# Two-layer hybrid network and mixture-of-experts block on one core: the conditioning vectors made by VectorE from a transposed modulation matrix instead of by TensorE

## The chip, the cores and the metric

One core of a Trainium2 chip runs the whole program. The metric is the device time in microseconds, median of three runs.

## What is computed

A first block of two hybrid layers (a convolution branch, a latent attention branch and a dilated attention branch, merged by gates) acts on x, 256 tokens of 1024 features. A second block follows: attention over tokens and a context, both modulated, then 32 experts of which each token uses four. All values are fp32. The change touches only how the modulation of the second block is made:

```python
mod_x = (jax.nn.silu(c) @ w_ada[l] + b_ada[l])[:, None, :]
mod_c = (jax.nn.silu(c_ctx) @ w_ada[l] + b_ada[l])[None, None, :]
sh1, sc1, gt1, sh2, sc2, gt2 = jnp.split(mod_x, N_MOD, axis=-1)
csh1, csc1, cgt1, csh2, csc2, cgt2 = jnp.split(mod_c, N_MOD, axis=-1)
h = modulate(rms_norm(x, g_attn[l]), sh1, sc1)        # h * (1 + sc1) + sh1
hc = modulate(rms_norm(ctx, g_attn[l]), csh1, csc1)
...
x = x + gt1 * (lat_mix @ w_o[l])
x = x + gt2 * moe_ffn(modulate(rms_norm(x, g_ffn[l]), sh2, sc2), ...)
```

c and c_ctx are vectors of 1024, w_ada is 1024 x 6144. The result does not depend on x, so it can be made at any time before the second block. Of c_ctx only the first 2048 columns (csh1, csc1) are used.

## The kernel before

Five engines run programs of their own, ordered by semaphores. SyncE (SP) issues all loads.

**The layers.** A layer is a list of units (UNITS). A weight tile of 2 MB is loaded into a ring of two slots, and cut into four quarters. ScalarE rounds a quarter into w_hi (L2037, `split_to`), GpSimd subtracts to get w_lo (L2138), and TensorE then runs three products (hi x hi, lo x hi, hi x lo, L1749 and L1759, `quarter`). Three quarters are buffered (PARTS), so a buffer is rounded anew as soon as TensorE has left it. Units up to PREP make the projections for the attentions: lora, dq, dk, dv, z, with the short latent units mq and mkv between them. VectorE normalizes and rotates their results (`normalize`, `rotate`, L2185 to L2188), TensorE turns them (`turn`, L1784), ScalarE copies them out of PSUM (`unflip`). ScalarE and VectorE wait for each other in these steps (squares, mean, root, reciprocal; "copied" for mkv).

**The jobs.** Twelve attention jobs follow (JOBS: four latent, eight dilated, j = 0 to 11). In step j TensorE makes the scores of job j (L1800, L1801, L1812), then waits for the probabilities of job j-1 (`values`, L1826 transposes, L1843 products) and between these runs quarters of the remaining weight tiles (`fill`). VectorE masks the scores of job j and takes the maximum (`mask`, L2357 to L2382), ScalarE does the exp (`exp`, L1999 to L2004), VectorE divides (`divide`, L2388 to L2395), and that releases the transposes of job j in the next step. The dilated jobs with odd j (5, 7, 9, 11) have two score steps: a second mask stands between the first and the exp. ScalarE copies the turned probabilities (`unflip_probs`, L2016). VectorE also does the convolution at j = 3 and 4 (L2342, L2345) and takes finished units out of PSUM. After the jobs come the merge (L1726), the output projection and the next layer.

**The conditioning before the change.** silu of c and c_ctx lies in SBUF as columns (`silu`, 8 chunks of 128 x 2, padded to 32). In each layer eight units of kind "ada" take 256 columns of w_ada each (1 MB, loaded by SP, L1652) and `ada_rows` (L715) multiplies them, four chunks side by side in the TensorE array. The result is a row, which ScalarE copies to `modrow` (L1961). After the first step of the jobs `pick` (L722) turns all rows of the layer with 16 small products (two passes each) into the PSUM tile mixed, and VectorE copies them to `mod` (L2442). The last 2048 columns are made in the attention block: four tiles of 2 MB in the ring (L647), eight half units between the last eight jobs (L715), and a second `pick` behind them, before the spreading of the sub norm (L891). The attention block has sixteen jobs (scores L823, maximum, exp L1173, division L1377 to L1384, transposes L833, values L845, copy L1390) and runs quarters of the projections and of w_o2 between them (`bfill`).

The calls that the prediction follows, in VectorE's order in a layer:

```python
for u in range(PREP):
    evacuate(l, u)
for j in range(NJ + 1):
    if j < NJ:
        mask(l, j, 0)
    for u in DONE_IN[j - 1] if j else ():
        evacuate(l, u)
    if j < NJ and len(STEPS[j]) == 2:
        mask(l, j, 1)
    if j < NJ:
        divide(l, j)
```

## Time and profile before

| | |
|---|---|
| time, median of 3 runs | 1980.42 us (1977.73 to 1983.41) |
| span of the profiled execution | 1975.8 us, 4.6 us less than that median |
| busy: TensorE, VectorE, ScalarE, GpSimd | 1885.4, 739.3, 581.0, 523.6 us |
| mean DMA rate | 285 GB/s |
| layer 1, layer 2, attention block, experts | 0 to 408, 408 to 810, 810 to 1041, 1041 to 1976 us |

The span is that of one execution; what the runs measure beyond it lies before its first and behind its last instruction, and between executions. A busy TensorE is an engine with a matmul in it, not one at its peak. GpSimd works in the layers only.

### The profile page before, as it was taken

The numbers are of one execution on the slowest core, as the hardware profiler recorded it, in microseconds if no ns is written. First come the engines' busy times: TensorE is split into PE (matmuls) and PEld (weight loads), VectorE is DVE, ScalarE is ACT, GpSimd is POOL, SyncE is SP. The second block draws the span as 40 slices with busy tenths as digits, with TensorE's granted clock in tenths as the row PEclk, the third lists the DMA queues.
The fourth block names the chain that finished last, engine by engine and source line by source line (L and its number), as shares of the span: only waits on it lengthen the run. The fifth ranks groups of instructions, "written<-read, shape, count | busy, mean of one in ns | idle before, by whom it ended". The sixth has DMA issues, their size and how long they took to land.

```text
span 1975.8 us, 26971 instructions
## 1 busy us (share of the span) xinstructions
PE 1885.4 (95%) x10996; PEld 1196.5 (61%) x10996; DVE 739.3 (37%) x1358; ACT 581.0 (29%) x1059; POOL 523.6 (27%) x220
## 2 busy tenths in 40 slices
PE   7999999989999899999999999999999999999997
PEld 6779989977799799844584444334334443433443
DVE  4785563447854643643533122111112211211112
ACT  4554455445554554423421111111001110110111
POOL 5766556767765558200000000000000000000000
PEclk9999999999999999999989999999999999999999
DMA  8556323545553334621558999999999999999995
GB/s 306 192 172 212 128 96 123 213 170 198 201 173 130 125 129 170 216 94 43 213 231 355 428 429 428 429 429 429 428 429 428 428 428 428 429 428 429 429 428 233
DMA packets 111413, 563.43 MB, mean 285 GB/s; under 512 B 4768, under 2 KB 24352, under 8 KB 86464
## 3 DMA queue, kind: packets, MB, share of 16 engines
q1 hardware_dynamic: 111328, 562.21, 71.2%
q8 instruction: 63, 1.03, 0.2%
q14 instruction: 22, 0.18, 0.0%
HBM read 561.15 MB, written 1.05 MB: 285 GB/s over the span
## 4 chain that ended last, share of the span: by engine, by line
PE 64%; DMA 28%; DVE 5%; ACT 1%; issue 1%; SPq 0%; DVEq 0%; ACTq 0%
DMA ring<-in_e_in_dram 28%; PE bank L1759 15%; PE score L964 11%; PE bank L1749 10%; PE bank L765 5%; PE mixed L1002 4%; PE bank L1726 3%; PE bank L796 1%; PE mixed L1843 1%; PE flip L1826 1%; DVE ring L2345 1%; PE bank L1025 1%; PE score L985 1%; PE score L823 1%; PE flip L1784 1%
## 5 line engine op out<-in xcount | busy, mean ns | idle before, releaser
L2138 POOL TENSOR_TENSOR w_lo<-ring,w_hi 128x1024 fp32r<-128x1024 f32 (+1 forms) x216 | 523.4, 2435 | 282.5 <-ACT w_hi L2037 281.8
L964 PE MATMUL score<-ring,space 128*64 128x512 f32 x2016 | 452.7, 594 | 38.6 <-DMA ring<-in_e_in_dram 37.5
L964 PEld LDWEIGHTS score<-ring,space 128*64 128x64 f32 x2016 | 141.5, 137 | 338.7 <-issue 248.6
L2037 ACT ACTIVATE w_hi<-ring 128x1024 fp32r<-128x1024 f32 (+1 forms) x216 | 226.5, 1050 | 218.8 <-PE bank L1759 119.3
L1759 PE MATMUL bank<-h_hi,w_hi 128*128 128x256 f32 x896 | 261.7, 292 | 0.0
L1759 PE MATMUL bank<-h_lo,w_hi 128*128 128x256 f32 x896 | 254.1, 284 | 0.0
L1759 PE MATMUL bank<-h_hi,w_lo 128*128 128x256 f32 x896 | 253.9, 283 | 0.0
L1002 PE MATMUL mixed<-ring,space 128*64 128x512 f32 x1024 | 228.1, 598 | 0.0
L1229 ACT ACTIVATE space<-space 128x512 f32<-128x512 f32 x32 | 20.2, 632 | 697.0 <-DVE space L1533 697.0
L1533 DVE TENSOR_SCALAR space<-score 128x512 f32<-128x512 f32 x32 | 22.2, 693 | 411.3 <-PE score L964 411.3
L1759 PEld LDWEIGHTS bank<-h_hi,w_hi 128*128 128x128 f32 x896 | 172.4, 192 | 4.5 <-issue 4.4
L1759 PEld LDWEIGHTS bank<-h_lo,w_hi 128*128 128x128 f32 x896 | 172.5, 193 | 0.1
L1759 PEld LDWEIGHTS bank<-h_hi,w_lo 128*128 128x128 f32 x896 | 172.2, 192 | 0.0
L1002 PEld LDWEIGHTS mixed<-ring,space 128*64 128x64 f32 x1024 | 71.0, 137 | 133.7 <-issue 131.4
L1749 PE MATMUL bank<-w_hi,h_hi 128*128 128x512 f32 (+1 forms) x320 | 131.9, 412 | 7.6 <-DVE h_lo L2194 7.6
L1546 DVE COPY space<-mixed 64x512 f32<-64x512 f32 x32 | 21.9, 684 | 297.5 <-PE mixed L1002 297.5
L1749 PE MATMUL bank<-w_hi,h_lo 128*128 128x512 f32 (+1 forms) x320 | 125.4, 392 | 0.0
L1749 PE MATMUL bank<-w_lo,h_hi 128*128 128x512 f32 (+1 forms) x320 | 125.1, 391 | 0.0
L1749 PEld LDWEIGHTS bank<-w_hi,h_hi 128*128 128x128 f32 x320 | 61.3, 192 | 24.5 <-issue 12.1
L1749 PEld LDWEIGHTS bank<-w_hi,h_lo 128*128 128x128 f32 x320 | 61.4, 192 | 12.1
L1749 PEld LDWEIGHTS bank<-w_lo,h_hi 128*128 128x128 f32 x320 | 61.5, 192 | 11.7 <-issue 1.0
L765 PE MATMUL bank<-ring,h 128*128 128x512 f32 (+1 forms) x160 | 64.5, 551 | 0.6 <-ACT h L1112 0.6
(349 smaller groups left out, 2341.0 us busy)
## 6 DMA issues: line engine op xcount, KB each, us to landing
ring<-in_e_in_dram SPq DMA_DIRECT2D x126, 2048.0 KB, 25.1
ring<-in_e_out_dram SPq DMA_DIRECT2D x64, 2048.0 KB, 22.1
ring<-in_w_in_dram SPq DMA_DIRECT2D x42, 2048.0 KB, 7.8
ring<-in_w_ada_dram SPq DMA_DIRECT2D x16, 1024.0 KB, 5.4
ring<-in_w_o_dram SPq DMA_DIRECT2D x6, 2048.0 KB, 7.9
ring<-in_w_qkv_dram SPq DMA_DIRECT2D x4, 2048.0 KB, 11.3
ring<-in_w_ada_dram SPq DMA_DIRECT2D x4, 2048.0 KB, 8.1
ring<-in_w_out_a_dram SPq DMA_DIRECT2D x2, 2048.0 KB, 8.0
```

The source lines that it names most:

```text
L765: ins = pe.matmul(b[:, 0:n], src[:, c, tt * P:(tt + 1) * P], w8[:, c, 0:n], start=c == 0, stop=c == DC - 1)
L796: ins = pe.matmul(b[:, i * T:(i + 1) * T], w8[:, c, m:m + P], mix[:, c, :], start=c == 0 and i == 0, stop=c == DC - 1, skip_group_check=True)
L964: ins = pe.matmul(score[HALF * blk:HALF * blk + HALF, which * W:(which + 1) * W], xs[:, 2 * j + r, HALF * hh:HALF * hh + HALF], wk[:, blk ...
L1002: ins = pe.matmul(mixed[HALF * side:HALF * side + HALF, :], actT[:, hh, a * P + HALF * half:a * P + HALF * half + HALF], ring[:, 4 + half, ...
L1229: act.activation(tanh_g[:, hh, :], glu[:, hh, :], ACT.Tanh, scale=GLU_ALPHA / 2).then_inc(glu_tanh, 1)
L1533: dve.tensor_scalar(glu[:, hh, :], score[:, 0:W], GLU_LIMIT, None, ALU.min).then_inc(glu_free, 1)
L1546: dve.tensor_copy(ys[0:HALF, hh, :], mixed[0:HALF, :])
L1726: ins = pe.matmul(b[:, i * T:(i + 1) * T], w_[:, c, m], y_[br][:, c, :], start=c == 0 and i == 0 and y_ is y_hi and w_ is hi, stop=c == 3 ...
L1749: ins = pe.matmul(b[:, 0:n], x_[:, c, t], w_[:, k % PARTS, i, 0:n], start=c == 0 and x_ is h_hi and w_ is w_hi, stop=c == DC - 1 and x_ is ...
L1759: ins = pe.matmul(b[:, half * T:(half + 1) * T], w_[:, k % PARTS, i, m:m + P], x_[:, c, :], start=c == 0 and half == 0 and x_ is h_hi and ...
L2037: act.activation(split_part(w_hi, k), raw_part(k), ACT.Copy).then_inc(hi_done, 1)
L2138: pool.tensor_tensor(split_part(w_lo, k), raw_part(k), split_part(w_hi, k), ALU.subtract).then_inc(lo_done, 1)
```

## The change

c and c_ctx come from the host as rows of 1024, repeated in all 128 partitions; w_ada comes transposed, as 48 blocks of 128 x 1024. A column of `mod` is then one VectorE instruction: the product of a block with the silu row, summed along the row (`tensor_tensor_reduce`). Both conditions together need 64 such sums: each layer does 16 steps of two (1 MB loaded per step). The blocks of the first 2048 columns are loaded twice in the first layer, for c_ctx and for c; the second layer does the other 4096, so nothing is left for the attention block. One step stands right behind the norm of x at the head of a layer, five in PREP, ten in jobs 0 to 9. One buffer holds the 1 MB; the loads after the first of a layer are issued by ScalarE. The tanh of the rows is made by ScalarE at the head of each layer, behind the last piece of h_hi. The ada units, their PSUM copies, `pick`, and their loads are gone.

```diff
-ADA_AFTER = {1: 1, 3: 2, 5: 3, 7: 4, 9: 5, 10: 6, 11: 7}
-ADA_LOAD = {2: 1, 4: 2, 6: 3, 8: 4, 10: 5, 12: 6, 13: 7}
-UNITS = [("ada", None, (0,))]
+UNITS = []
...
+COND = 2
+ROWS = [[(1, COND * n) for n in range(8)] + [(0, COND * n) for n in range(8)], [(0, COND * n) for n in range(8, 24)]]
+NROWS = 16
+ROWS_AFTER = {LONG_AT[0] + 1: 1, LONG_AT[1] + 1: 2, LONG_AT[7] + 1: 3, LONG_AT[9] + 1: 4, PREP - 1: 5}
+ROWS_LOAD = {LONG_AT[0]: 1, LONG_AT[1]: 2, LONG_AT[3]: 3, LONG_AT[8]: 4, LONG_AT[10]: 5}
+ROWS_JOB = 6
+CTX_STEPS = 8
...
-BUNITS += [("ada", (7, 8, 11, 12)[n], (n,)) for n in range(4)]
...
-BHALVES = [4] + [2] * NGQA + [2] * 7 + [1]
+BHALVES = [4] + [2] * NGQA + [1] * 7 + [0]
...
-            pe.wait_ge(mixed_free, MIXED0 + M_ADA + 1)
-            for n in range(4):
-                pe.wait_ge(bank_free[BBANK[BADA + n]], bfreed(BADA + n))
-                ins = pick(pe, bmodrow[:, n, :], 8 * n)
-            ins.then_inc(mixed_done, 1)
...
+        def rows_of(l, k):
+            a = ROWS[l][k][1]
+            return w_ada[a:a + COND].rearrange("a p k -> p a k")
...
+                def first_rows(l):
+                    if l:
                         sp.wait_ge(free_of(MERGED - 1), freed(l - 1, MERGED - 1))
+                    sp.dma_start(c_row, c_in[:, 0:D]).then_inc(c_loaded, 16)
+                    if l == 0:
+                        sp.dma_start(ctx_row, c_in[:, D:2 * D]).then_inc(c_loaded, 16)
+                    sp.dma_start(ada_sb, rows_of(l, 0)).then_inc(ada_landed, 16)
...
@@ block.tensor, after the first step of the jobs @@
-                        pe.wait_ge(mixed_free, l * NM + 1)
-                        for n in range(ADAS):
-                            ins = pick(pe, modrow[:, n, :], 8 * n)
-                        ins.then_inc(mixed_done, 1)
...
@@ block.scalar @@
-            act.activation(tanh_z[:, 0:2 * DC], cvec[:].rearrange("p c b -> p (c b)"), ACT.Tanh,
-                           scale=0.5).then_inc(ctanh, 1)
+            def row_tanhs(l):
+                act.wait_ge(c_loaded, 32 if l == 0 else 48)
+                if l == 0:
+                    act.activation(row_tanh[:, 1, :], ctx_row, ACT.Tanh, scale=0.5).then_inc(ctanh, 1)
+                act.activation(row_tanh[:, 0, :], c_row, ACT.Tanh, scale=0.5).then_inc(ctanh, 1)
+            def load_rows(l, k):
+                act.wait_ge(ada_used, l * NROWS + k)
+                act.dma_start(ada_sb, rows_of(l, k)).then_inc(ada_landed, 16)
...
                     split_to(l, min(n + 1, PARTS))
                     stream_high(l, n, normed_x)
-                evacuate(l, 0)
-                for u in range(HEAD, PREP):
+                row_tanhs(l)
+                for u in range(PREP):
                     if u in QUARTER:
                         k = QUARTER[u]
                         for q in range(4):
                             split_to(l, k + q + 1 + PARTS)
                             if (u, q) in TURN:
                                 unflip(l, NORMED.index(TURN[u, q]))
+                        if u in ROWS_LOAD:
+                            load_rows(l, ROWS_LOAD[u])
                         evacuate(l, u)
...
                     if j > 0:
                         unflip_probs(l, j - 1, 0)
+                    if ROWS_JOB + j < NROWS:
+                        load_rows(l, ROWS_JOB + j)
                     if j < NJ and len(STEPS[j]) == 1:
                         exp(l, j)
...
@@ block.vector @@
+            def silu_rows(l):
+                for i, row in ((1, ctx_row), (0, c_row)):
+                    if i == 0 or l == 0:
+                        dve.wait_ge(ctanh, l + 2 - i)
+                        dve.scalar_tensor_tensor(out=row, in0=row_tanh[:, i, :], scalar=1.0, in1=row, op0=ALU.add,
+                                                 op1=ALU.mult).then_inc(row_ready, 1)
+                dve.wait_ge(row_ready, l + 2)
+            def use_rows(l, k):
+                b, a = ROWS[l][k]
+                dve.wait_ge(ada_landed, 16 * (l * NROWS + k + 1))
+                for i in range(COND):
+                    ins = dve.tensor_tensor_reduce(out=ada_sb[:, i, :], in0=ada_sb[:, i, :], in1=(c_row, ctx_row)[b],
+                                                   scale=0.5, scalar=0.0, op0=ALU.mult, op1=ALU.add,
+                                                   accum_out=mod[:, a + i, b:b + 1])
+                ins.then_inc(ada_used, 1)
...
+                silu_rows(l)
+                use_rows(l, 0)
                 for u in range(PREP):
                     evacuate(l, u)
+                    if u in ROWS_AFTER:
+                        use_rows(l, ROWS_AFTER[u])
                 for j in range(NJ + 1):
                     if j < NJ:
                         mask(l, j, 0)
                     for u in DONE_IN[j - 1] if j else ():
                         evacuate(l, u)
+                    if ROWS_JOB + j < NROWS:
+                        use_rows(l, ROWS_JOB + j)
                     if j < NJ and len(STEPS[j]) == 2:
                         mask(l, j, 1)
                     if j < NJ:
                         divide(l, j)
...
-                        dve.wait_ge(mixed_done, l * NM + 1)
-                        dve.tensor_copy(mod[:, bass.ds(l * 4 * ADAS, 4 * ADAS), :],
-                                        mixed[:, 0:8 * ADAS].rearrange("p (c b) -> p c b", b=2)).then_inc(mixed_free, 1)
```

## Rows read from the trace of the kernel before

**Rows 1.** Stages: busy us (instructions) of PE, PEld, DVE, ACT, POOL; PEclk, DMA share, GB/s.

```profile
60.00:160.00 100.00, 98.91 (x527) 77.42 (x526) 83.54 (x97) 51.31 (x81) 70.66 (x29) 1.00 0.56 190
...
1195.00:1485.00 290.00, 272.33 (x1333) 111.82 (x1333) 49.58 (x110) 29.19 (x64) 0.00 (x0) 1.00 1.01 429
```

**Rows 2.** Timeline of TensorE in PREP: start, us, line, operation [idle before].

```profile
41.80 1.07 PE L715 MATMUL mixed<-ring,silu 128*32 128x256 f32 x16
```

**Rows 3.** Timeline of TensorE: turning of the rows, and what follows it.

```profile
189.92 3.63 PE L722 MATMUL mixed<-cst,ring 128*128 128x2 f32 x32
...
195.18 1.06 PE L1826 MATMUL flip<-cst,space 128*128 128x128 f32 x4
...
996.11 6.58 PE L722 MATMUL mixed<-cst,space 128*128 128x2 f32 x32
```

**Rows 4.** Stages around the turning in both layers; the granted clock stands after POOL.

```profile
160.00:200.00 40.00, 39.81 (x331) 37.63 (x331) 17.41 (x29) 20.16 (x39) 23.88 (x11) 0.96 0.54 185
...
560.00:600.00 40.00, 39.81 (x318) 37.64 (x318) 17.88 (x26) 18.20 (x31) 24.75 (x11) 0.92 0.54 185
```

**Rows 5.** VectorE with two SBUF inputs (groups by line: xcount, busy, mean ns), then GpSimd.

```profile
L2213 DVE TENSOR_TENSOR latent_r<-space,latent_r 128x1024 fp32r<-128x1024 f32 x1 | 3.2, 3208 | 0.0
...
L2213 DVE TENSOR_TENSOR latent_r<-ring,latent_r 128x1024 fp32r<-128x1024 f32 x1 | 1.2, 1215 | 0.0
...
289.86 3.39 POOL L2138 TENSOR_TENSOR w_lo<-ring,w_hi 128x1024 fp32r<-128x1024 f32 x1
```

**Rows 6.** Timelines of ScalarE and GpSimd: table load, split at the head, 128x1024 operation.

```profile
2.40 1.28 ACT L1912 ACT_TABLE_LOAD   x1 [2.40 <-DMA cvec<-in_c_dram]
...
25.23 9.06 POOL L2138 TENSOR_TENSOR w_lo<-ring,w_hi 128x832 fp32r<-128x832 f32 x4 [3.14 <-ACT w_hi L2037]
...
279.12 1.05 ACT L2048 ACTIVATE latent_r<-space 128x1024 fp32r<-128x1024 f32 x1
```

**Rows 7.** DMA issues by line: xcount, KB each, median us from issue to landing.

```profile
ring<-in_w_ada_dram SPq DMA_DIRECT2D x16, 1024.0 KB, 5.4
```

**Rows 8.** Timeline of the first layer's jobs: transposes, copies, masks, divisions.

```profile
181.75 0.69 DVE L2295 SCALAR_TENSOR_TENSOR space<-ring,bank 128x512 f32<-128x512 f32 x1 [0.72 <-ACT ring L1984]
...
247.80 0.66 PE L1826 MATMUL flip<-cst,space 128*128 128x128 f32 x4
...
260.18 1.15 DVE L2395 TENSOR_SCALAR space<-space 128x768 f32<-128x768 f32 x2
...
261.82 0.66 PE L1826 MATMUL flip<-cst,space 128*128 128x128 f32 x4
...
275.03 0.66 PE L1826 MATMUL flip<-cst,space 128*128 128x128 f32 x4
...
280.07 0.59 ACT L2016 ACTIVATE space<-flip 128x512 f32<-128x512 f32 x1
...
282.05 0.75 DVE L2371 SCALAR_TENSOR_TENSOR space<-cst,score 128x256 f32<-128x256 f32 x2 [1.32 <-PE score L1812]
...
286.51 1.15 DVE L2395 TENSOR_SCALAR space<-space 128x768 f32<-128x768 f32 x2
...
289.47 0.66 PE L1826 MATMUL flip<-cst,space 128*128 128x128 f32 x4
...
302.67 0.66 PE L1826 MATMUL flip<-cst,space 128*128 128x128 f32 x4
...
314.88 0.66 PE L1826 MATMUL flip<-cst,space 128*128 128x128 f32 x4
```

**Rows 9.** Timeline of the attention block: scores, copy of the mixed rows, diagonal.

```profile
956.94 1.13 PE L823 MATMUL score<-space 64*128 64x512 f32 x4
...
962.40 1.13 PE L823 MATMUL score<-space 64*128 64x512 f32 x4
...
962.64 0.28 DVE L1390 COPY space<-mixed 128x128 f32<-128x128 f32 x1
...
997.03 1.29 DVE L1398 TENSOR_TENSOR space<-cst,space 128x512 f32<-128x512 f32 x2
```

142 lines of the change are left out of this document (41 added, 101 removed).

## The prediction

> **What bounds the kernel now.** I read the table of stages first, then the waits, then the timelines of single stretches. The span falls into two dense layers (0 to 408 us and 408 to 810), an attention block (810 to 1041) and 32 experts (1041 to 1976). In a layer TensorE is busy 98.9 of 100 us while the conditioning rows are made, and VectorE, second, is busy 83.5, GpSimd 70.7 [rows 1]. So there a microsecond taken from TensorE is a microsecond gained, if VectorE, GpSimd and ScalarE still deliver in time. Among the experts the DMA engines are full (429 GB/s) and TensorE waits for them [rows 1]; the first tile of the second expert is only asked for when TensorE has used the first one's, so whatever moves the start of the experts moves the end by as much, and nothing else there is touched by the change.
>
> **What is removed from TensorE.** Seven of a layer's eight products of 16 matmuls lie between full-rate work and cost 1.0 us each (1.07 less the overlap, [rows 2]): 7.0 us a layer. The eighth stands at the layer's head, where TensorE waits for h_lo anyway: 0. The 32 small matmuls that turn the rows take 3.6 us in a layer [rows 3]. Around them the granted clock falls to the 1.2 GHz level: a mean of 0.96 over 40 us is 3.2 us at that level in the first layer, 0.92 is 6.4 us in the second [rows 4], and half of that is lost time, 1.6 and 3.2 us. What TensorE did just before is 3.6 us of matmuls of two columns. Gross gain: 7.0 + 3.6 + 1.6 = 12.2 us in the first layer, 13.8 in the second.
>
> In the attention block each of the last eight jobs loses 1.0 us of products. TensorE's own period of 5.46 us would be 4.46. But scores, maximum, exp, division and the copy of the mixed rows form one chain on VectorE: from the end of one job's scores (956.94 + 1.13) to the end of that copy (962.64 + 0.28) are 4.85 us, so the period becomes about 4.9 and seven periods give 3.9 us [rows 9]. The turning there takes 6.6 us (996.11 to 1002.69, [rows 3]), and what follows it needs the first diagonal of VectorE, ready half way through the 1.29 us from 997.03 [rows 9]: 1002.6 less 997.8 is 4.8 us. The four row copies of ScalarE and four 2 MB loads lie beside other work: 0.5 us at most. Block: -9.2 us. The small first load and tanh are gone from the start: -0.4 us (estimate; between 0 and the 1.3 us of the table load of [rows 6]).
>
> **What is added to VectorE.** Per layer 32 products with a row sum, 128x1024, both inputs in SBUF, and one or two multiplications of the same size. The trace has no such sum; nearest is a 128x1024 TENSOR_TENSOR with both inputs in SBUF, 1.22 us free and 3.21 us when GpSimd runs [rows 5]. I take 1.25 us free, 2.5 a pair, with bounds 1.2 and 3.2 for one. The other side of the same collision: GpSimd's split, 2.4 us as a rule, took 3.39 beside it [rows 5]. The Trainium skill (SBUF — State Buffer, "Who interferes with whom") says that a VectorE instruction with two SBUF inputs and a GpSimd instruction that reads SBUF exclude each other for their whole length. By that rule this change puts its work on the one port that the layers already crowd; the two rows agree with it.
>
> **The head of a layer.** ScalarE now makes tanh of two rows (one in the second layer) between the last h_hi piece and the fourth quarter of the weights. Each is like the 128x1024 ACTIVATE of 1.05 us, and the table changes to tanh, 1.28 us [rows 6]: 3.4 us. GpSimd took that quarter at 25.23, and four quarters in 9.06 us without a pause [rows 6], while TensorE ran without a wait: the cover is nil. The silu multiplications and the first pair then hold GpSimd off for four times 1.25 us, of which TensorE's 2.7 us a quarter against GpSimd's 2.3 absorb about half. The table back to sqrt (1.28) and the wait of ScalarE's queue for the first pair (new: its DMA issue stands behind that use, and squares, root and the next split behind the issue) fall partly in the same gap. In all 5.5 us, in the second layer 4.7 (one row less, 1.05, partly covered). Bounds 2 and 8. The other five pairs up to the jobs go into idle time of VectorE except where GpSimd is held or ScalarE waits for the shared "copied" order: 2.5 us a layer (0 to 6). So up to the jobs: -7.0 + 5.5 + 2.5 = +1.0 and -7.0 + 4.7 + 2.5 = +0.2.
>
> **The jobs.** This is the term that decides. In job j ScalarE asks for the next 1 MB only after it has copied out the first turned probabilities of job j-1, and VectorE does the pair between its first mask and the division of job j, on which TensorE's next transposes wait with nothing else queued ahead of them. A 1 MB load of w_ada took 5.4 us to land, in 1 KB pieces [rows 7]; the new ones are 4 KB pieces, and I take 4.5 (bounds 3.5 and 6, more where a 2 MB tile is under way). From the transposes to the end of that copy 1.3 us, issue 0.4, landing 4.5, pair 2.5: VectorE is free of the pair 8.7 us after the transposes, and 1.3 (division alone) or 5.6 to 5.8 us (second mask, exp, division) later the probabilities are ready.
> - Jobs with one step: transposes follow each other every 13.2 us on average (195.18 to 247.80 in four jobs), so 10.0 is in time; a pair that meets the lock twice makes it 12 to 13: about 0.5 us each for jobs 2 and 4, 1.5 for job 3, whose load meets a weight tile (estimates).
> - Job 5: its division ends at 260.18 + 1.15 and the transposes run at 261.82, a slack of 0.5 us, in a stretch where VectorE has hardly a pause; a pair of 2.5 us and the backlog of job 4 give 4.0 us.
> - Job 7: ScalarE comes to the copy only at 280.07, 5.0 after the transposes at 275.03. Copy 0.6, issue 0.4, landing 4.5, pair 2.5: 288.1 in place of 282.05 for the second mask, 5.6 more is 293.7, against 289.47: 4.3 us.
> - Job 9: 8.7 + 5.8 = 14.5 against 314.88 - 302.67 = 12.2: 2.3 us.
> - Job 0: VectorE's last step before it ends at 182.4, the pair of step 5 at 184.9; only then is the next load issued; it lands at 189.8, pair and division with one GpSimd split between give 196. TensorE, without the turning, would be there at 191.2 (189.92 + 1.3) and came at 195.18: 4.8 us of new wait.
> Together 0.5 + 0.5 + 1.5 + 4.0 + 4.3 + 2.3 + 4.8 = 17.9 us of new waits a layer [rows 3, 8]. Waits of 4 to 5 us should cost a stretch at the 1.2 GHz level: 1.6 us, the smaller stretch of [rows 4]. 19.5 less the gain of turning and clock (3.6 + 1.6; 3.6 + 3.2) is +14.3 and +12.7 us. Bounds for the waits: 4 us a layer (job 7 alone) and 32.
>
> **The sum.** +1.0 + 14.3 + 0.2 + 12.7 - 9.2 - 0.4 = +18.6 us. The profiled execution has a span of 1975.8 us; the runs' median 1980.42 is 4.6 above it, taken as constant. 1975.8 + 18.6 + 4.6 = 1999.0 us.
>
> **The rivals.**
> A, faster: the cover holds. If a load lands in 3.5 us and the pairs hit GpSimd's pauses, only job 7 stalls (4 us a layer) and the head costs 2 to 3 us. Two layers: 2 x (-7.0 + 3 + 1) + 2 x 4 - 5.2 - 6.8 = -10, with the block -9.6: 1961 us. For it: VectorE is idle nearly half of the jobs' time, and the DMA engines over half. Against it: the pair stands ahead of the division, not in the idle time. It decides below about 8 us of waits a layer.
> B, much slower, by the lock: every pair meets the split on both halves (3.2 for each 1.25, +3.9 a pair), about 8 pairs a layer reach TensorE: +2 x 16 above the forecast after what slack takes: 2028 us. This is the outcome of the Trainium skill's rule above if GpSimd always has work queued. Against it: when TensorE waits, GpSimd soon waits too and frees the port.
> C, no change: waits of 8 to 11 us a layer pay back just the gain: 1981 us.
> D, that it doesn't do what it says: the products could be two passes each (2.4 us free); then as B.
>
> **How the numbers follow.** Forecast 0.50, B and D 0.22, A 0.19, C 0.09. About 0.3% (6 us) is what a measurement tells from no change. The forecast's own range, from waits of 12 to 24 us a layer, is 1987 to 2011. The range for 8 in 10 takes in B and most of C, and cuts A and the far end of B: 1966 to 2030. Faster 0.20, same 0.09, slower 0.71.
>
> **What would show it.** TensorE matmuls of L715 and L722 gone and no low clock after 190 us; at the head a GpSimd start 3 us later; VectorE pairs of 2.5 to 5 us, many starting at a landing; new waits of TensorE for VectorE's probabilities at jobs 0, 5, 7 and 9 in both layers; attention jobs at 4.9 us; the experts' rate unchanged. It is wrong if the pair's end is not the last thing before the transposes, or if the loads land much sooner or later than 4.5 us.

## The result and the profile after

The changed kernel takes 2032.35 us (median of 4 runs, 2028.59 to 2033.83) against 1980.5 for the kernel before: a ratio of 1.0261, 95% interval 1.0248 to 1.0275. The direction was forecast, the size was not: +52 us in place of +18.6, beyond the range. The profiled execution has a span of 2026.8 us, 51.0 more than before. All spans below are of one execution each; those of the kernel before lie between 1975.7 and 1984.3 us, with 1975.8 near the low end, and the kernels that leave something out ran once or twice (the control of experiment 7 four times), so spans some 5 us apart are not told apart.

The page of the changed kernel: busy times, GpSimd and the granted clock in 40 slices, and the chain that ended last.

```profile
span 2026.8 us, 26233 instructions
...
PE 1866.4 (92%) x10580; PEld 1189.6 (59%) x10580; DVE 905.6 (45%) x1485; ACT 579.2 (29%) x1045; POOL 548.5 (27%) x220
...
PEclk8999889999998999999998999999999999999999
...
PE 44%; DMA 30%; DVE 19%; ACT 3%; issue 2%; POOL 1%; DVEq 0%; SPq 0%; ACTq 0%
```

VectorE has 166 us more to do, of which the sums are 127. GpSimd runs the same 216 splits as before and yet is busy for 25 us more: it is held up.

Where the 51 us arise is read from landmarks that both timelines have: the first turning of a layer (end of the head), the last turning of the projections, the last transposes of the jobs, the end. Each number is how much a stage takes longer than in the kernel before.

| | head 1 | projections 1 | jobs 1 | head 2 | projections 2 | jobs 2 | block and experts | sum |
|---|---|---|---|---|---|---|---|---|
| forecast | +5.1 | -4.5 | +14.3 | +4.7 | -4.5 | +12.7 | -9.2 | +18.6 |
| measured | +5.0 | +0.8 | +26.9 | +3.6 | +2.4 | +21.2 | -8.9 | +51.0 |

The heads and the attention block came as forecast. The projections and the jobs did not. The answers to [rows 1] show it (columns as there): TensorE loses 3.75 of 100 us in the projections where it had lost 1.1, and the experts are as before.

```profile
60.00:160.00 100.00, 96.25 (x439) 75.61 (x438) 87.98 (x100) 50.30 (x80) 73.55 (x30) 0.98 0.51 178
...
1245.00:1535.00 290.00, 272.51 (x1335) 112.04 (x1335) 49.74 (x110) 29.18 (x64) 0.00 (x0) 1.00 1.01 429
```

What TensorE waited for in the changed kernel (total, times, longest). Transposes (L1782) did not wait for a division at all in the kernel before:

```profile
PE flip L1782 <- DVE space L2365: 27.8, 5, 8.6
PE flip L1782 <- DVE space L2369: 17.6, 8, 4.5
PE bank L1705 <- DVE h_lo L2146: 12.8, 4, 6.1
PE flip L1740 <- ACT space L1902: 7.9, 8, 2.1
...
PE bank L1705 <- POOL w_lo L2095: 6.8, 7, 3.0
```

VectorE's groups by shape (x count, busy, mean ns): the sums, and the divisions behind them.

```profile
L2181 DVE CUSTOM_DVE_ANT_0 ring<-ring 128x1024 f32<-128x1024 f32 x48 | 91.0, 1932 | 42.2 <-DMA ring<-in_w_ada_dram 41.7 <-DVE space L2234 0.3 <-DVE space L2229 0.2
L2181 DVE CUSTOM_DVE_ANT_0 ring<-ring,space 128x1024 f32<-128x1024 f32 x16 | 35.7, 2268 | 7.2 <-DMA ring<-in_w_ada_dram 6.7 <-DVE space L2234 0.3 <-DVE space L2229 0.2
L2369 DVE TENSOR_SCALAR space<-space 128x384 f32<-128x384 f32 x16 | 24.4, 1564 | 0.3
L2364 DVE TENSOR_SCALAR space<-space 128x128 f32<-128x128 f32 x16 | 19.1, 1192 | 0.3
L2181 DVE DVE_READ_ACCUMULATOR2_ANT mod<- 128x1 f32 x64 | 5.0, 79 | 0.0
```

A free sum is 1.22 us with 0.08 for reading the accumulator, as forecast; the mean is 2.0. The divisions of these two shapes took 417 and 284 ns in the kernel before and now take 1564 and 1192. Nothing in them was changed.

One job is enough to see how. Timeline of the changed kernel, job 2 of the first layer (start, us, engine, line; the part in brackets is idle time before it):

```profile
222.28 0.60 PE L1782 MATMUL flip<-cst,space 128*128 128x128 f32 x4
...
222.93 0.38 ACTq L1871 DMA_DIRECT2D ring<-in_w_ada_dram  x1
...
229.10 2.02 DVE L2181 CUSTOM_DVE_ANT_0 ring<-ring 128x1024 f32<-128x1024 f32 x1 [3.17 <-DMA ring<-in_w_ada_dram]
...
231.06 3.40 DVE L2181 CUSTOM_DVE_ANT_0 ring<-ring 128x1024 f32<-128x1024 f32 x1
...
234.59 2.15 DVE L2364 TENSOR_SCALAR space<-space 128x128 f32<-128x128 f32 x1
...
227.66 2.38 POOL L2095 TENSOR_TENSOR w_lo<-ring,w_hi 128x1024 fp32r<-128x1024 f32 x1 [2.95 <-ACT w_hi L1990]
230.72 2.65 POOL L2095 TENSOR_TENSOR w_lo<-ring,w_hi 128x1024 fp32r<-128x1024 f32 x1 [0.68 <-ACT w_hi L1990]
234.12 2.54 POOL L2095 TENSOR_TENSOR w_lo<-ring,w_hi 128x1024 fp32r<-128x1024 f32 x1 [0.74 <-ACT w_hi L1990]
...
237.90 1.09 PE L1782 MATMUL flip<-cst,space 128*128 128x128 f32 x4 [3.64 <-DVE space L2365]
```

The load lands 6.2 us after its issue. The first sum is issued at 229.10, GpSimd's split ends at 230.04, and the sum ends 1.1 us later. A split is issued at 230.72 and takes its turn when the first sum ends; the second sum, issued at 231.06, waits for all of it: 3.40 us is its own 1.22 and GpSimd's 2.2. The next split is issued at 234.12, and the first piece of the division stands behind that one: 2.15 us for 0.28. So 14.5 us pass from the issue of the load to the end of the division, where the forecast had 4.5 + 2.5 + 1.3 and "a pair that meets the lock twice" as a mishap. In the kernel before, the division of this job ended 5.6 us behind the transposes and had 5.9 us of slack; now it ends 15.2 behind them, 9.6 later: 5.9 are absorbed, 3.7 are the new wait.

TensorE's clock pays once more. Windows of the first 800 us, the kernel before and then the changed one (granted clock behind POOL's busy time):

```profile
0.00:800.00 800.00, 769.32 (x5535) 678.54 (x5536) 446.50 (x691) 400.58 (x655) 517.53 (x218) 0.99 0.49 170
```

```profile
0.00:800.00 800.00, 705.46 (x4705) 618.64 (x4706) 590.64 (x788) 371.13 (x607) 495.64 (x198) 0.95 0.51 182
```

Rounded as they are, 0.99 is 8 to 24 of 800 us at 1.2 GHz and 0.95 is 72 to 88: 48 to 80 us more. Much of it stands at the new waits: 186 to 226 us, around the 8.6 us wait of job 0, has 0.87.

### The profile page after: what moved, and what is told of

The parts are those of the page before. It is cut to its first block, busy times and chain, and to the rows that moved or that the text cites. A ratio compares the mean times of both kernels' runs of the same rounds, so it can differ in the third digit from the quotient of the medians.

```text
span 2026.8 us, 26233 instructions
## 1 busy us (share of the span) xinstructions
PE 1866.4 (92%) x10580; PEld 1189.6 (59%) x10580; DVE 905.6 (45%) x1485; ACT 579.2 (29%) x1045; POOL 548.5 (27%) x220
## 4 chain that ended last, share of the span: by engine, by line
PE 44%; DMA 30%; DVE 19%; ACT 3%; issue 2%; POOL 1%; DVEq 0%; SPq 0%; ACTq 0%
DMA ring<-in_e_in_dram 26%; PE score L932 11%; PE bank L1715 8%; PE bank L738 5%; PE mixed L970 4%; DVE ring L2181 4%; DMA ring<-in_w_ada_dram 3%; PE bank L1682 3%; PE bank L1705 3%; DVE space L2137 1%; DVE space L2219 1%; PE flip L1782 1%; PE score L953 1%; DVE space L2138 1%; PE bank L993 1%
## 5 line engine op out<-in xcount | busy, mean ns | idle before, releaser
L2095 POOL TENSOR_TENSOR w_lo<-ring,w_hi 128x1024 fp32r<-128x1024 f32 (+1 forms) x216 | 548.3, 2552 | 317.2 <-ACT w_hi L1990 316.8
L1715 PE MATMUL bank<-h_hi,w_hi 128*128 128x256 f32 x896 | 267.7, 299 | 3.5 <-POOL w_lo L2095 3.5
L1715 PE MATMUL bank<-h_hi,w_lo 128*128 128x256 f32 x896 | 258.6, 289 | 0.0
L1715 PEld LDWEIGHTS bank<-h_lo,w_hi 128*128 128x128 f32 x896 | 176.6, 197 | 0.6 <-issue 0.5
L1705 PE MATMUL bank<-w_hi,h_hi 128*128 128x512 f32 (+1 forms) x320 | 137.3, 429 | 19.8 <-DVE h_lo L2146 12.8
L1505 DVE COPY space<-mixed 64x512 f32<-64x512 f32 x32 | 21.9, 684 | 294.5 <-PE mixed L970 294.5
L970 PEld LDWEIGHTS mixed<-ring,space 128*64 128x64 f32 x1024 | 70.7, 137 | 132.8 <-issue 130.4
L2181 DVE CUSTOM_DVE_ANT_0 ring<-ring 128x1024 f32<-128x1024 f32 x48 | 91.0, 1932 | 42.2 <-DMA ring<-in_w_ada_dram 41.7
L1705 PEld LDWEIGHTS bank<-w_hi,h_hi 128*128 128x128 f32 x320 | 62.9, 196 | 38.3 <-issue 15.7
L1782 PE MATMUL flip<-cst,space 128*128 128x128 f32 x192 | 35.3, 303 | 45.5 <-DVE space L2365 27.8
```

What stands on the lines that cost most here:

```text
L970: ins = pe.matmul(mixed[HALF * side:HALF * side + HALF, :], actT[:, hh, a * P + HALF * half:a * P + HALF * half + HALF], ring[:, 4 + half, ...
L1505: dve.tensor_copy(ys[0:HALF, hh, :], mixed[0:HALF, :])
L1705: ins = pe.matmul(b[:, 0:n], x_[:, c, t], w_[:, k % PARTS, i, 0:n], start=c == 0 and x_ is h_hi and w_ is w_hi, stop=c == DC - 1 and x_ is ...
L1715: ins = pe.matmul(b[:, half * T:(half + 1) * T], w_[:, k % PARTS, i, m:m + P], x_[:, c, :], start=c == 0 and half == 0 and x_ is h_hi and ...
L1782: ins = pe.transpose(flip[:, i * P:(i + 1) * P], pr[:, w, c * P:(c + 1) * P], ident)
L2095: pool.tensor_tensor(split_part(w_lo, k), raw_part(k), split_part(w_hi, k), ALU.subtract).then_inc(lo_done, 1)
```

## The experiments

The theories to tell apart. **Place**: the pair and the landing of its load stand ahead of the division, and any work of that length there would cost this. **Collision**: a sum with two SBUF inputs and a split of GpSimd exclude each other, and that makes the price wherever the pair stands. **Gain**: what is taken from TensorE was worth less than forecast. A kernel that leaves something out does not compute the result; it serves for its time alone. The table of stages at the end of this section holds all runs; the spans are compared with 1975.8 us of the kernel before.

**1. The gain alone.** No loads, tanh, silu or sums.

```diff
-                act.dma_start(ada_sb, rows_of(l, k)).then_inc(ada_landed, 16)
...
-                row_tanhs(l)
...
-                    ins = dve.tensor_tensor_reduce(...)
-                ins.then_inc(ada_used, 1)
+                dve.sem_inc(ada_used, 1)
...
-                silu_rows(l)
```

> The changed kernel without the conditioning itself: no rows are loaded, no tanh, no silu multiplication and no sum is made, and mod keeps its zeros. What is left is the gain alone. By the prediction's terms it is 12.2 us in the first layer, 13.8 in the second, 9.2 in the attention block and 0.4 at the start, 35.6 in all: a span of 1940 us against 1975.8 before. If it is right, what the change adds cost 87 us and not 54, and the error lies wholly in what is added. The rival is that part of the gain was never there (products of the removed kind beside other waits): then the span is above 1950.

Measured: ratio 0.9869 (0.984 to 0.9897), span 1952.1 us. The gain is 23.7 us, not 35.6, and the rival is right: 12 us were never there. The block gives its 8.9; the layers give 7.8 and 7.0 in place of 12.6 and 13.8. A wait of TensorE in this kernel, and a window of its first layer's jobs, say where the rest goes:

```profile
PE flip L1737 <- ACT space L1898: 6.8, 8, 2.1
```

```profile
240.00:280.00 40.00, 36.09 (x290) 32.04 (x289) 21.85 (x51) 19.11 (x32) 18.02 (x9) 0.91 0.31 106
```

The removed products had stood between quarters and turnings and covered ScalarE's copies of what was turned before (waits of 2.2 us in all in the kernel before). And the clock gave nothing back: a mean of 0.91 is 7 us at 1.2 GHz in the jobs of the first layer, where the kernel before has none from 200 to 320 us (1.00) but 3.2 us behind the turning of the rows. In the second layer the stretch from 630 to 680 us has 0.93, again 7 us, and 500 to 540 us, in the projections, 0.96. What brings these stretches at waits of some 2 us that the kernel before has too (the masks behind the convolution: 3.5 us in all before, 3.6 now) is open.

**2. Loads without sums, and sums without loads.**

```diff
# loads only: the sums stay for the first pair of a layer, otherwise
+                    dve.sem_inc(ada_used, 1)
...
# sums only: the loads behind the first of a layer are left out, and
-                dve.wait_ge(ada_landed, 16 * (l * NROWS + k + 1))
+                dve.wait_ge(ada_landed, 16 * (l + 1))
```

> The changed kernel with all loads and all of VectorE's waits for them, but without the sums behind the first pair of each layer (mod keeps zeros there). If the landing of the loads is what makes the division late, most of the waits for probabilities stay (25.8 us of TensorE in the first layer's jobs, 19.6 in the second's in the changed kernel) and the span is over 2000 us. If the sums and what they collide with do it, the waits fall below 5 us a layer, job 7 being the only one left, and the span is near 1960: 1940 and twice the head's 5.5 and twice 3 to 5.

> The changed kernel with all sums, but without the loads behind the first of each layer: the sums run on what lies in the buffer, never wait, and mod holds wrong values. If landings are the cause, waits for probabilities fall below 8 us a layer and the span is near 1975. If the sums are it (32 a layer at up to 3.4 us, and the divisions behind them slowed by GpSimd), over half of the waits stay, 12 us a layer or more, and the span is 1995 to 2020. Over 2020: the landing costs nothing at all.

Measured: 1974.0 and 1989.5 us. Against the gain alone the loads (with the heads) cost 21.9 us, the sums (with the heads) 37.4; both together are 74.7. The heads stand in both and are 10 us. So 12 and 27 become 65: neither is the cause alone. With slack like the 5.9 us of job 2 above, most of what one of them adds to the division's lateness would be absorbed, and what both add would not; that is the reading that fits, and no run shows it by itself.

**3. The same time with one SBUF input.** The sums are replaced by plain reductions of the same block (which also write no product back).

```diff
-                    ins = dve.tensor_tensor_reduce(out=ada_sb[:, i, :], in0=ada_sb[:, i, :], in1=(c_row, ctx_row)[b],
-                                                   ..., accum_out=mod[:, a + i, b:b + 1])
+                    ins = dve.tensor_reduce(mod[:, a + i, b:b + 1], ada_sb[:, i:i + 1, :], AX.X, ALU.add)
```

> The changed kernel with every sum replaced by a plain reduction of the same 128x1024 block: one SBUF input in place of two, about the same free time (a reduction of that size shows 1.22 us in the trace of the kernel before), at the same place, with the same loads and waits; mod holds wrong values. If a shared SBUF access with GpSimd is the cause, the pairs take 2.5 us, GpSimd's splits stay at 2.4 us, and the waits for probabilities fall to the 13 to 18 us of the prediction or below: span 1985 to 2000. If the place of the pair ahead of the division and the time of landing are the cause, the span stays above 2015.

Measured: span 1999.4 us, 27.4 less than the changed kernel, inside what the collision theory gave. The group of the reductions, and GpSimd's splits:

```profile
L2181 DVE TENSOR_REDUCE mod<-ring 128x1 f32<-128x1024 f32 x64 | 75.0, 1214 | 60.0 <-DMA ring<-in_w_ada_dram 59.4 <-DVE space L2232 0.5
...
L2095 POOL TENSOR_TENSOR w_lo<-ring,w_hi 128x1024 fp32r<-128x1024 f32 x208 | 507.7, 2454 | 272.0 <-ACT w_hi L1990 271.8
```

None of the 64 reductions was held, and the splits are back at the 2450 ns of the kernel before (2569 in the changed one). The divisions, still late, are still blocked (1298 ns for 384 columns). My forecast of +18.6 us is close to this kernel's +23.6, and this is the kernel whose sums are never held. But the closeness is in part luck: the gain is 23.7 us here and not 35.6, and what is added 47.3 and not 54.2.

**4. Another place.** The pair behind the division; the same with one-input reductions; and the head moved into the projections besides.

```diff
+                    if j < NJ:
+                        divide(l, j)
                     if ROWS_JOB + j < NROWS:
                         use_rows(l, ROWS_JOB + j)
-                    if j < NJ and len(STEPS[j]) == 2:
-                        mask(l, j, 1)
-                    if j < NJ:
-                        divide(l, j)
```

> The changed kernel with one edit: in the jobs the pair of sums stands behind the division of the job in VectorE's order, and no longer ahead of it. All sums, loads and values are as in the changed kernel. If landing, pair and blocked division in one chain make the loss of the jobs, the waits for probabilities (25.8 and 19.6 us of TensorE in the two layers of the changed kernel) fall to about 5 us a layer, the divisions go back to 0.3 to 0.4 us each, and the span is 1952 (what is left without any conditioning) + 9.6 (head, both layers) + 9 (the pairs before the jobs) + 10 = 1981 us, 1975 to 1990. If the collisions of VectorE and GpSimd cost by themselves, wherever the pairs stand, it stays above 2010.

> Pair behind the division, and each sum replaced by the plain reduction of the same block (one SBUF input; mod holds wrong values). Against the run with the pair behind the division it tells what the second SBUF input costs once the pair is off the path. If the collision costs only where somebody waits for the pair or for the split beside it, 0.8 us for each of the five pairs before the jobs and 1 to 2 at the head remain, some 10 us in two layers: a span near 1971. If nearly nothing of it is left, the two spans agree within 4 us.

Measured: 2028.7 us with real sums (ratio 1.0246, 1.0222 to 1.0269), no better than the changed kernel; 1975.3 with one-input reductions. My expectation for the first was wrong by 48 us. The sums at this place (first group), and the timeline of one job (second fence):

```profile
L2181 DVE CUSTOM_DVE_ANT_0 ring<-ring 128x1024 f32<-128x1024 f32 x48 | 118.1, 2495 | 23.1 <-DMA ring<-in_w_ada_dram 22.6 <-DVE space L2234 0.3 <-DVE space L2229 0.2
...
L2369 DVE TENSOR_SCALAR space<-space 128x384 f32<-128x384 f32 x16 | 6.0, 417 | 0.3
```

```profile
276.24 3.39 DVE L2181 CUSTOM_DVE_ANT_0 ring<-ring 128x1024 f32<-128x1024 f32 x1
...
279.56 0.28 DVE L2380 SCALAR_TENSOR_TENSOR space<-mixed,space 128x128 f32<-128x128 f32 x1
...
279.94 0.63 PE L1782 MATMUL flip<-cst,space 128*128 128x128 f32 x4 [1.79 <-issue]
```

The divisions are free again (417 ns), but a sum now takes 2.5 us in the mean, and what is late is the gating (L2380) behind the pair, whose end frees the PSUM tile mixed for the next values: TensorE goes on 0.4 us after its start (the profile names no releaser there; `values` waits for mixed_free). I had not listed what else stands behind the pair in VectorE's order.

For the head, tanh, silu and the first pair go behind the second and third long unit of the projections:

```diff
-                row_tanhs(l)
...
+                        if u == LONG_AT[1]:
+                            row_tanhs(l)
...
-                silu_rows(l)
-                use_rows(l, 0)
...
+                    if u == LONG_AT[1] + 1:
+                        silu_rows(l)
```

> As the run before, and besides the tanh of the rows, the silu multiplication and the first pair stand no longer at the head of a layer but behind the second and third long unit of the projections; tanh and silu use the buffer of the loads. The output is the whole result. The head's 5.7 and 3.9 us should go: the first turning of the layer comes at 37.4 us as without conditioning, not at 43.3. The tanh's table loads and the moved pair give back 1 to 2 us a layer: 1981 - 9.6 + 3 = 1974 us of span, 1968 to 1982. If ScalarE or GpSimd have no slack there either, all of it comes back and the span equals that of the run before.

Measured: 2050.8 us, 1.0379 (1.0354 to 1.0404). The heads do vanish (the first turning at 38.2 us, as before), and the projections lose 16.5 and 14.5 us in their place: TensorE's turnings wait 25.0 us for ScalarE's copies (6.8 in the gain alone). Whether the table loads and tanh or the pairs among the normalizations make these late was not separated.

> The changed kernel with the division left out in the four latent jobs of each layer (one instruction of 16 columns keeps the signal), so their probabilities are not normalised. In the changed kernel these divisions take 5.4 us a job, 1.4 in the kernel before. If the blocked division is on the path, each of the eight latent jobs gains its 5.4 us and a part of the low clock: span 2026.8 - 8 x 5.4 = 1984, at most 2000. If the division only fills time in which something else is late, the gain is under 11 us (8 x 1.4) and the span above 2015.

```diff
-                    for w in range(2):
-                        dve.tensor_scalar(pr[:, w, 0:P], ...)
-                        ins = dve.tensor_scalar(pr[:, w, P:384], ...)
+                    ins = dve.tensor_scalar(pr[:, 1, P:P + 16], pr[:, 1, P:P + 16], st[:, 15:16], None, ALU.mult)
```

Measured: 2019.9 us, 6.9 less, under the 11 that I had set as the bound. What was left in the place of the latent divisions:

```profile
L2363 DVE TENSOR_SCALAR space<-space 128x16 f32<-128x16 f32 x8 | 16.5, 2063 | 0.3
```

The 16 columns take 2063 ns: the small instruction is held in the division's place, and 16.5 of the 33.0 us that the latent divisions took are still there. (They are the 128 and 256 columns, 4.1 us a job; my 5.4 counted the 384 columns of the dilated jobs, which are still held, 1687 ns.) So the run shows that a short instruction is held as long, and does not show what the blocked division costs.

**5. The end of the step**, behind the gating and the convolution.

```diff
                     if j in (3, 4):
                         convolve(l, j - 3)
+                    if ROWS_JOB + j < NROWS:
+                        use_rows(l, ROWS_JOB + j)
```

> The changed kernel with one edit: in the jobs the pair of sums is the last thing in VectorE's step, behind the division, behind the gating multiplication of the job before and behind the convolution. All sums and values are there. The run with the pair directly behind the division left the gating behind the pair, and its trace shows TensorE's transposes of the next job starting 0.4 us after that gating. If the place was its whole fault, the jobs lose little now: a span of 1952 + 17 (head and pairs before the jobs as there) + 2 x 8 = 1985 us, 1978 to 1995. If the collision with GpSimd sets the price wherever the pair stands (each sum 2.5 us in place of 1.2 and the work behind it late), the span stays above 2010.

> The same place at the end of the step, each sum replaced by the plain reduction of the same block (one SBUF input; mod holds wrong values). The difference to the run with real sums is what the second SBUF input costs at this place. By the place theory both agree but for the head and the pairs before the jobs (8 to 10 us): a span near 1975. By the collision theory they differ by over 30 us, as the runs with the pair ahead of the division (27) and directly behind it (53) did.

Measured: 2023.9 us (1.0248, 1.0231 to 1.0265) with real sums, 1976.1 with one-input reductions. A pair of real sums here holds off the next mask; exp waits for the mask, and behind exp in ScalarE's order stands the copy of turned probabilities that TensorE needs. Timeline, VectorE's pair and mask, then ScalarE, then TensorE:

```profile
270.98 3.21 DVE L2181 CUSTOM_DVE_ANT_0 ring<-ring 128x1024 f32<-128x1024 f32 x1
...
274.12 3.39 DVE L2181 CUSTOM_DVE_ANT_0 ring<-ring 128x1024 f32<-128x1024 f32 x1
...
277.44 1.26 DVE L2345 SCALAR_TENSOR_TENSOR space<-cst,score 128x128 f32<-128x128 f32 x6
...
279.94 0.61 ACT L1957 ACTIVATE space<-space 128x384 f32<-128x384 f32 x1 [7.32 <-DVE space L2356]
...
282.72 1.12 PE L1799 MATMUL mixed<-space 128*64 128x128 f32 x8 [3.89 <-ACT space L1969]
```

Three places, three spans within 5 us of each other, and three different steps that came late. The place decides who waits, the blocked pair decides how long: with one input the places are 1999.4, 1975.3 and 1976.1.

**6. As long, but with one input.** Each sum is one plain reduction over all 2048 columns of the buffer.

```diff
-                    ins = dve.tensor_tensor_reduce(...)
+                    ins = dve.tensor_reduce(mod[:, a + i, b:b + 1], upper[:, 4 * D:6 * D].rearrange("p (a k) -> p a k", a=1),
+                                            AX.X, ALU.add)
```

> Pair directly behind the division, as in the run of that place, but each sum replaced by one plain reduction over the whole 1 MB buffer (2048 columns, one SBUF input; mod holds wrong values): some 2.4 us each, 4.8 a pair, which is what a pair of real sums took there on average (153 us for 32 pairs), with no second input. If the collision costs only by making the pair longer, the span is that of the real sums, 2028 us, within 6. If the rest of the loss is on the other side (GpSimd's split and other instructions of VectorE held up, pairs of 6.8 us where the mean hides them), it is near 1995, between the 1975 of the short reductions and 2028.

Measured: 2006.7 us, with a pair of 4.6 us (2279 ns twice; a pair of real sums takes 5.0 here in the mean). Of the 53 us by which real sums exceed short reductions at this place, the mean length gives 31. The other 22 were open: also the collision, or the two-input sum itself.

**7. The other party.** The sums stay; behind the first eight quarters of the first layer GpSimd's splits are cut to 16 columns of 512, 0.38 us in place of 2.45.

```diff
+                    n = None if l == 0 and k < 8 else 16
-                    pool.tensor_tensor(split_part(w_lo, k), raw_part(k), split_part(w_hi, k),
+                    pool.tensor_tensor(split_part(w_lo, k)[:, :, 0:n], raw_part(k)[:, :, 0:n], split_part(w_hi, k)[:, :, 0:n],
```

> The kernel before with GpSimd's subtraction cut from 512 columns to 16 of each row behind the first eight quarters (the rest of w_lo keeps stale values, so the layers' products are not the reference's). It is the control for the next two: what GpSimd's splits cost the kernel before. TensorE waits for w_lo only 3 us in it, so the span should fall by 5 to 15 us, to 1960 to 1970.

> The changed kernel with the same cut of GpSimd's subtraction; all sums with two SBUF inputs, all loads and places are kept. If the loss is the collision with GpSimd, every sum is back at 1.2 us and every division at 0.3 to 0.4, and the changed kernel is no more than 15 us slower than the control (in the uncut pair: 51). If the length and place of the work on VectorE and the loads set it, the difference stays above 35 us.

> The kernel with the pair behind the division, with the same cut. With one-input sums this place cost nothing against the kernel before (1975.3 against 1975.8 us), with real sums 53 us. If the collision is the whole difference, it is here within 5 us of the control; if a real sum costs more than its 1.2 us in some other way, it is 20 us or more behind.

Measured: the kernel before 1967.1 us (0.9949, 0.9929 to 0.9968), the changed one 1953.3 (0.9884, 0.9855 to 0.9912), the one with the pair behind the division 1944.0 (0.9826, 0.9798 to 0.9855). VectorE's groups in the second of these:

```profile
L2182 DVE CUSTOM_DVE_ANT_0 ring<-ring 128x1024 f32<-128x1024 f32 x48 | 57.3, 1231 | 51.6 <-DMA ring<-in_w_ada_dram 51.2 <-DVE space L2235 0.3
```

The 384-column divisions are back at 417 ns. With the same sums, loads, waits and places, the change is worth 13.8 us and not a loss of 51, and with the pair behind the division 23.1. So the loss needs GpSimd's long splits: the short ones take 64.8 us from it in the changed kernel (51.0 + 13.8), 76.0 with the pair behind the division (52.9 + 23.1). The 22 us are part of it: 61 of the 64 two-input sums take 1.2 us.

Not all of the 64.8 us is the collision of the new work. A short split also delivers w_lo 2 us sooner (TensorE's waits for it fall from 10.3 us to 2.7), and it frees the older instructions of VectorE. The projections show it: against the kernel before they gain 7.0 and 7.4 us, where the kernel without any conditioning work gains 3.7 and 2.1 and the control 1.0 and 1.0. So some 7 us of the 64.8 (8.6 less the control's 2.0) would be there without a single sum. The gain alone with short splits was not measured.

**8. A faster kernel.** The prediction put a stretch at 1.2 GHz down to the run of two-column matmuls that turns the rows. In the kernel before, these are now spread behind the three quarters of the first job step, 8, 8 and 16 of them.

```diff
                     while taken[0] < sum(QUARTERS[:j + 1]):
                         fill(l)
+                        if j == 0:
...
+                            ins = pick(pe, modrow[:, n, :], 8 * n)
-                        for n in range(ADAS):
-                            ins = pick(pe, modrow[:, n, :], 8 * n)
```

> The kernel before with one edit: in each layer the turning of the conditioning rows is no longer one run of 32 small matmuls of two columns (3.6 us) behind the third quarter of the first job step, but 8, 8 and 16 of them behind its three quarters. The work is the same. If the run of two-column matmuls is what takes TensorE to its 1.2 GHz level there (3.4 us at that level in the first layer, 6.8 in the second), these stretches go and 1.7 + 3.4 = 5 us are gained: 1975 us, 0.26% below the kernel before. If the level falls for another reason (the small matmuls of the attention itself), the time is unchanged within 0.1%.

Measured: 1974.74 us, ratio 0.9974 (0.9964 to 0.9985): faster than both kernels, and 0.26% is what was expected. Timeline of the first layer, then the windows that answer to [rows 4]:

```profile
184.65 0.95 PE L722 MATMUL mixed<-cst,ring 128*128 128x2 f32 x8
...
188.41 0.95 PE L722 MATMUL mixed<-cst,ring 128*128 128x2 f32 x8
...
192.18 1.84 PE L722 MATMUL mixed<-cst,ring 128*128 128x2 f32 x16
```

```profile
160.00:200.00 40.00, 39.81 (x345) 37.65 (x344) 17.84 (x28) 20.55 (x39) 24.40 (x11) 1.00 0.53 185
560.00:600.00 40.00, 39.81 (x345) 37.67 (x344) 18.22 (x27) 19.79 (x37) 25.16 (x11) 1.00 0.54 185
```

The same 3.7 us of small matmuls, and the granted clock is 1.00 where it was 0.96 and 0.92. By the landmarks the stretch gives 1.1 us in the first layer, lost again at a later job, and 3.2 in the second: 2.7 us of span between the two profiled executions. Two windows limit what this shows. The first is of this kernel, later in the first layer, where the kernel before has 1.00; the second is of the control of experiment 7, whose turning is one run of 32 again (188.67 us, 3.63 us long):

```profile
240.00:280.00 40.00, 35.74 (x293) 32.02 (x291) 24.37 (x46) 17.68 (x30) 21.74 (x9) 0.96 0.38 135
```

```profile
160.00:200.00 40.00, 39.81 (x346) 37.65 (x345) 10.10 (x27) 19.81 (x37) 2.69 (x10) 1.00 0.48 169
```

In the first layer the 3.2 us at 1.2 GHz have not gone but moved to a later job, and the same single run of small matmuls can pass at 1.00. So the run of 32 is not enough by itself to bring the clock down; only the second layer shows the stretch gone for good. That the kernel with the spread turning is faster is measured; that the clock is the whole reason is not.

All runs by stage, in us against the kernel before (span of the profiled execution in the last column):

| | head 1 | proj. 1 | jobs 1 | head 2 | proj. 2 | jobs 2 | rest | span |
|---|---|---|---|---|---|---|---|---|
| changed kernel | +5.0 | +0.8 | +26.9 | +3.6 | +2.4 | +21.2 | -8.9 | 2026.8 |
| gain alone | -0.9 | -3.7 | -3.2 | -0.3 | -2.1 | -4.6 | -8.9 | 1952.1 |
| loads only | +4.8 | -1.6 | +2.5 | +3.6 | -1.7 | +0.2 | -9.6 | 1974.0 |
| sums only | +5.1 | +2.5 | +4.0 | +3.6 | +2.0 | +3.9 | -7.4 | 1989.5 |
| one input | +4.7 | -1.7 | +14.3 | +2.0 | -0.4 | +12.2 | -7.5 | 1999.4 |
| no latent division | +4.9 | +3.7 | +18.8 | +3.5 | +2.6 | +19.1 | -8.5 | 2019.9 |
| behind the division | +4.6 | +2.1 | +21.3 | +3.6 | +2.1 | +28.5 | -9.3 | 2028.7 |
| the same, one input | +5.3 | -2.4 | +3.2 | +2.1 | -0.8 | +2.0 | -9.9 | 1975.3 |
| the same, long, one input | +3.7 | -0.3 | +15.5 | +3.6 | -0.5 | +17.3 | -8.4 | 2006.7 |
| behind it, head moved | -0.1 | +16.5 | +28.0 | -0.1 | +14.5 | +23.8 | -7.6 | 2050.8 |
| end of the step | +3.9 | +2.2 | +23.2 | +3.5 | +2.4 | +21.7 | -8.8 | 2023.9 |
| the same, one input | +4.0 | -1.8 | +0.7 | +2.1 | -0.3 | +3.7 | -8.1 | 1976.1 |
| before, short splits | -0.2 | -1.0 | -3.5 | -0.9 | -1.0 | -3.2 | +1.1 | 1967.1 |
| changed, short splits | +4.3 | -7.0 | +0.1 | -2.0 | -7.4 | -0.4 | -10.1 | 1953.3 |
| behind, short splits | +4.4 | -7.0 | -3.8 | -1.7 | -7.4 | -8.7 | -7.6 | 1944.0 |
| before, turning spread | +0.5 | 0.0 | -0.1 | 0.0 | 0.0 | -3.2 | +0.1 | 1973.1 |

## Why the prediction was right and where it was wrong

The forecast missed by 32.4 us: 11.9 in the gain, 20.5 in what is added. Two of its steps failed. "I take 1.25 us free" for every sum took the free price where half of them were held, and let the division pass free as well; and seven products, the turning and its clock were booked as a pure gain, with nothing put down for what they covered.

**Attention block, -9.2: right in the sum** (-8.9 in the changed kernel and in the gain alone). The jobs' period, of which [rows 9] gave 4.9 by VectorE's chain, is 4.72, so the periods gave more than the forecast's 3.9 us, about 0.74 each, and the turning and the rest less than its 5.3. Timeline of the changed kernel, scores of two jobs:

```profile
1029.64 1.13 PE L798 MATMUL score<-space 64*128 64x512 f32 x4
1034.36 1.13 PE L798 MATMUL score<-space 64*128 64x512 f32 x4
```

**Head, 5.5 and 4.7: right in size** (5.0 and 3.6 with the start; against the gain alone 5.9 and 3.9). ScalarE does the table and the tanh of two rows where it had split the fourth quarter, GpSimd takes the quarter at 27.26 where it would have at 24.2 (25.23 of [rows 6] less the 1.0 us by which the start is now earlier), and TensorE waits:

```profile
23.09 1.28 ACT L1865 ACT_TABLE_LOAD   x1
...
26.30 2.77 ACT L1990 ACTIVATE w_hi<-ring 128x832 fp32r<-128x832 f32 x3
...
27.26 11.46 POOL L2095 TENSOR_TENSOR w_lo<-ring,w_hi 128x832 fp32r<-128x832 f32 x4 [6.19 <-ACT w_hi L1990]
...
29.78 0.71 PE L1705 MATMUL bank<-w_hi,h_hi 128*128 128x416 f32 x1 [2.97 <-POOL w_lo L2095]
```

The wait is 2.97 us. The rest is a part that I had not listed, more time at 1.2 GHz (20 to 60 us has 0.89, in the kernel before 0.95), in the place of parts that I had put too high: a total that fits by luck, made of other terms.

**Seven products at 1.0 us, and the clock: wrong step.** "Lie between full-rate work" [rows 2] was read as "each is a gain". They were also the cover of ScalarE's copies ahead of the turnings. Six of the seven stand in the projections as the landmarks cut them; the seventh follows 0.2 us behind the last turning and counts to the jobs. So 6.0 us were to come in the projections, and 3.7 and 2.1 came: 4.6 us went to the turnings' waits in the two layers, and in the second layer some 1.6 to a new stretch at 1.2 GHz. In the jobs the seventh product, the turning and its clock [rows 3, 4] were to give 6.2 and 7.8 us and gave 3.2 and 4.6: the time at 1.2 GHz did not go away with the turning, it stands at later jobs (experiment 1).

**The other five pairs, 2.5 a layer: the size was off.** Against the gain alone they cost 4.5 us in either layer; as one-input reductions they would cost 2.0 and 1.7.

**The jobs: right mechanism, mis-sized term.** The chain was named as it is (copy, issue, landing, pair, division, transposes) and so were new waits at jobs 0, 5, 7 and 9, though not their sizes (in the first layer 8.6, 2.6, 0.7 and 2.5 us for 4.8, 4.0, 4.3 and 2.3); 19.5 us a layer were forecast as the added part, 30.1 and 25.8 were measured. The forecast's three terms of the chain were all low: landing 4.5 us (the page gives a median of 5.2 over 30 issues, 6.2 in the job shown), a pair 2.5 (4.1 in the mean with the reading of the accumulator), a division 1.3 (3.1 in the job shown). The pair failed by the step "I take 1.25 us free": of the two rows for this operation, 1.22 and 3.21 [rows 5], I took the free one as the value for every pair and the held one as a bound. GpSimd is busy 70.7 of 100 us in the projections [rows 1], and that share was the number to weigh the two rows with: of the 64 sums 33 came free and 31 were held, 17 of them for over 3.3 us in all. More rows lay in the trace of the kernel before than the two that I used. In the rotation of the projections VectorE multiplies two SBUF inputs too; first the group in the kernel before, then the same with short splits:

```profile
L2186 DVE TENSOR_TENSOR space<-space,cst 128x64 f32<-128x64 f32 x14 | 33.6, 2400 | 0.0
```

```profile
L2187 DVE TENSOR_TENSOR space<-space,cst 128x64 f32<-128x64 f32 x14 | 3.0, 218 | 0.0
```

These 0.2 us were held for a whole split every time. And VectorE's 83.5 busy us of 100 [rows 1] are 38.3 with short splits: over half of its work in the projections was time spent held, so the engine that the change loads was crowded by what it shares with GpSimd more than by its own work.

And the three jobs that I gave 2.5 us together (2, 3 and 4) lost 12.8 in the first layer, because the division itself collides once it comes late. That collision shows in no row of the kernel before, since the division then ran in a pause of GpSimd (job 2: 215.7 to 216.7 us, the next split is issued at 216.5).

The clock term, 1.6 us a layer, was low as well: 48 to 80 us more at 1.2 GHz in two layers, of which less than half is lost, since part of the time TensorE stood still.

**The rivals.** B named the outcome (2028 us; its own sum, 2 x 16 above 1999.0, is 2031) and the cause, the lock, but its size by luck: it held both halves of every pair, 3.9 us more for each, and measured are 1.6 more in the mean (4.1 against 2.5), with no pair over 3.3 us on both halves. The rest came through the divisions, which B did not name. What spoke against it, "when TensorE waits, GpSimd soon waits too and frees the port", is seen only with the pair ahead of the division, where a sum takes 2.0 us in the mean; behind the division it takes 2.4. What the Trainium skill (SBUF — State Buffer, "Who interferes with whom") says of which instructions take part in the lock fits all runs: two SBUF inputs collide with GpSimd's reads (a sum 1.22 or 3.4 us), a tensor_reduce never does (64 of 64 at 1.2 us), and a tensor_scalar can (0.28 to 1.19 us), each held for the whole of the other's instruction. A, faster, was right of a kernel without the collision alone: 13.8 us faster than its control. D did not occur: a sum is one pass of 1.22 us.

**What stays open.** How the 64.8 us divide between sums held, other VectorE instructions held, splits held, w_lo delivered sooner and the clock behind each wait; only the whole was measured. No run put the pairs into GpSimd's pauses by a wait; with one-input reductions, which are never held, the best place only equals the kernel before (1975.3 and 1976.1 us), so such an order would have to mend the heads too before it wins.

## What to carry to other kernels

Before work is moved to an engine that is "half idle", count what it shares: the busy share of the other user is a first measure of how often each new instruction will be held, and it is held for up to the whole length of the other's. The engine's own busy share can mislead, because time spent held counts as busy (83.5 of 100 us here, 38.3 once the other's instructions are short). List every step that stands behind the new work in its engine's order and its slack, because moving the work only picks another of them. And before a product is booked as a gain, ask what it was covering: here a third of the gain was not there.

## What the runs showed of the hardware that I had not expected

- The second of two instructions in a row is held most. 16 of the 17 sums over 3.3 us are the second of their pair: the next split was issued while the first ran, and took its turn between them. The first of these pairs took 1.2 us (nine times) to 2.9.
- How long an instruction is held does not depend on its own length: 16 columns of a division took 2.06 us, a product of 128x64 2.40 us where it is 0.22 free.
- Unchanged instructions can become four times as slow without a change in their own code: 384 columns from 417 to 1564 ns, only by coming at another time.
- Around the two-column matmuls, 3.7 us in all, TensorE's granted clock was 0.96 and 0.92 over 40 us when they came in one run, and 1.00 in three pieces with 2.8 us of full-rate quarters between them. But in the kernel with short splits one run passed at 1.00, and in the spread kernel the first layer's stretch at 1.2 GHz came later instead (240 to 280 us: 0.96).
